# Tokens stationary in the last product, and one 512-column matmul over high and low operand in the front and the latents

## The chip, the cores and the metric

The kernel runs on one core of one Trainium2 chip. The time is device microseconds (us) of that core. The kernel before was run three times: 1950.55, 1955.09 and 1958.80 us, median 1955.09 us. The engines are named as in the profile: PE (TensorE matmuls), PEld (its weight loads), DVE (VectorE), ACT (ScalarE), POOL (GpSimd) and SP (the engine that issues most DMAs).

## The reference, cut to what matters

Two blocks follow one another on 256 tokens of width 2048, all in float32. The first normalises `x`, multiplies it by a wide input matrix, runs three mixers and an output product, and then attends to a memory of 256 rows. The second runs a pooling layer and a latent-attention layer on the tokens and on a context of 256 rows. What the change touches:

```
# front: memory's keys and values; the first columns of the mixers' input product
k, v = split(rms_norm(mem, mem_norm_g) @ wkv)
p = rms_norm(x, mix_norm_g) @ w_in
...
# every layer of the second block; the gate of the context is not used in the last layer
shift, scale, gate = split(silu(c) @ ada_w[i] + ada_b[i], 3)
c_q, c_kv, k_r, g = split(h @ mla_w_in)
o = attend(...)                                  # 16 heads of 128
y = (o * silu(g)) @ mla_w_out                    # 256 x 2048
x = x + gate * rms_norm_2(y, post_norm[i])       # the output, last layer
```

## The kernel before, in words

**Layout.** Activations lie transposed: a tile of `BIG` is 128 features by 256 tokens. A weight product reads its matrix in chunks of 512 rows by 512 columns (1 MB, two DMAs into `RAW`), and splits each chunk: ACT rounds it into `HI` (`act_high`, L306), DVE subtracts that from the raw values into `LO` (`dve_low`, L316), a half of 128x1024 elements at a time. The operand is split too, `x[:, 0, :]` the high part and `x[:, 1, :]` the low part, 256 tokens each (`XS`, `PS`). Each 128x128 block of weights gives three matmuls into one PSUM bank (`pe_block`, L489): high weights by high operand (L503), high weights by low operand (L504), low weights by high operand (L505). With one sequence (`seqs == 1`) each moves 256 columns, with two sequences (latent tokens and context) 512.

**Order.** Each engine has a queue of its own, written out by hand, and semaphores join them. `HI` and `LO` have two slots, so that the work on a chunk runs one to two chunks ahead of PE. PE signals `chunk_done` after each half of a chunk and `tile_done` after a finished output tile. A finished bank is evacuated: by ACT for the kinds `copy1`, `copy2`, `gain1` (`act_evac`), by DVE for `add1`, and by both for `gate1` (ACT writes a sigmoid of the bank, DVE multiplies it with the bank). A bank is used again only after that (`pe_bank`, L507).

**Beside it** the modulation vectors `silu(c) @ ada_w` and `silu(c_ctx) @ ada_w` are summed on DVE: 192 units of 512 KB, each with four operations of 128x512 (two k by two vectors, L427 and L431, `dve_unit`). After eight units PE adds the partitions up (`pe_ada`, L440, two matmuls with `PICK`). The last four slabs, units 160 to 191, are the gates of the last layer, and their units run in the attention stage.

**Stages the change touches.** *Front* (0 to 260 us): products `kv` (8 chunks), `win_a` (24), `win_b` (4, three tiles wide), all `copy1`; a barrier (`stage_end`) closes it. *Latents* (1338 to 1563 us): `cq` (4 chunks, `copy1`), `mg01` (8, `gate1`), `ckv`, `kr` (two sequences), `mg23` (8, `gate1`), then a barrier. *Pairs* (1563 to 1847 us): attention of two heads beside the products `uq` and `ukv` of the next two, nine rounds of some 32 us; in the ninth the first three chunks of the last product `mo` lie beside the attention. *mo* (1847 us to the end): the other 13 chunks, weights stationary, 256 tokens moving, result features by tokens. ACT takes each tile out twice (times the gate, L385, and squared, L388), DVE sums the squares (L2929), PE turns the input `x` (L2889, eight turns of four transposes) and the result (L2899, four calls of eight transposes) back to tokens by features and sums the squares over partitions (L2970), and DVE forms `x + y * rstd` in eight pieces (L2950), each sent out by SP.

## Time and profile before

| | us |
|---|---|
| median of three runs | 1955.09 |
| time of the profiled execution | 1950.72 |
| its span, first to last instruction | 1948.9 |
| PE busy | 1802.2 |
| DVE busy | 1416.7 |
| ACT busy | 817.5 |
| mean granted TensorE clock, share of full | 0.964 |

A row of a timeline gives start, duration, engine, line, operation, output and inputs, shapes and a count, and in brackets how long the engine had been idle and what released it. The ends of matmuls are modelled, so PE's pace is read from the starts of matmuls, not from their durations. The granted clock is a share of 2.4 GHz.

### The profile page before, as it was taken

The page shows a single profiled execution, that of the slowest core. Times are in us where ns is not written, and L with a number is a line of the kernel's source. Part 1 is how long each engine was busy: PE and PEld are TensorE (multiplying, and loading weights), DVE is VectorE, ACT ScalarE, POOL GpSimd, SP SyncE. Part 2 cuts the span into 40 slices and gives each one's busy share as a digit, 9 for nine tenths or more (in the row PEclk, how much of TensorE's full clock was granted, in tenths as well). Part 3 has the DMA queues.
Part 4 walks back from the last instruction along what each step waited for, and adds up shares of the span by engine and source line. Part 5 has one row for each costly group of instructions (what it writes and reads, how often), then busy time and mean ns, then how long its engine had stood idle before and what let it go on. Part 6 is the DMA issues. An engine that isn't in the chain of part 4 may idle for free.

```text
span 1948.9 us, 27051 instructions
## 1 busy us (share of the span) xinstructions
PE 1802.2 (92%) x10641; PEld 1547.9 (79%) x10641; DVE 1416.7 (73%) x2242; ACT 817.5 (42%) x1294; POOL 7.2 (0%) x18
## 2 busy tenths in 40 slices
PE   6999988997888888999999999997989999999897
PEld 6899988987777777877777777775978966667697
DVE  5788758778899677887688768777772677777443
ACT  6544365624435444233332223224453444444353
POOL 1000000000000000000000000000000000000000
PEclk9999999999899989999999999998999999999999
DMA  6577744535566344345455536553442453434243
GB/s 213 191 260 260 229 154 152 184 97 171 193 227 227 109 150 126 113 141 173 135 197 183 191 129 204 185 192 107 130 138 76 145 170 110 136 109 150 78 152 98
DMA packets 169000, 311.11 MB, mean 160 GB/s; under 512 B 14908, under 2 KB 23464, under 8 KB 168872
## 3 DMA queue, kind: packets, MB, share of 16 engines
q1 hardware_dynamic: 162176, 305.70, 48.0%
q10 hardware_dynamic: 6248, 3.62, 0.7%
q8 instruction: 84, 1.38, 0.3%
q14 instruction: 44, 0.36, 0.1%
q0 software_dynamic: 448, 0.06, 0.0%
HBM read 307.23 MB, written 2.10 MB: 159 GB/s over the span
## 4 chain that ended last, share of the span: by engine, by line
PE 52%; DVE 7%; ACT 3%; issue 1%; DMA 0%; DVEq 0%; ACTq 0%
PE bank L503 15%; PE bank L504 15%; PE bank L505 15%; DVE w_low L316 2%; PE bank L2627 2%; PE bank L2626 1%; DVE ada_acc L431 1%; PE bank L2646 1%; PE bank L449 1%; ACT w_high L306 1%; PE bank L2637 1%; DVE big L682 1%; DVE big L2470 0%; DVE big L2469 0%; DVE operand L677 0%
## 5 line engine op out<-in xcount | busy, mean ns | idle before, releaser
L503 PE MATMUL bank<-operand,w_high 128*128 128x256 f32 (+1 forms) x2704 | 872.4, 323 | 73.1 <-DVE w_low L316 43.5
L504 PE MATMUL bank<-operand,w_high 128*128 128x256 f32 (+1 forms) x2704 | 860.2, 318 | 0.0
L505 PE MATMUL bank<-operand,w_low 128*128 128x256 f32 (+1 forms) x2704 | 860.1, 318 | 0.0
L503 PEld LDWEIGHTS bank<-operand,w_high 128*128 128x128 f32 x2704 | 529.5, 196 | 130.7 <-DVE w_low L316 50.2
L316 DVE TENSOR_TENSOR w_low<-raw,w_high 128x1024 fp32r<-128x1024 f32 (+4 forms) x416 | 454.1, 1127 | 187.9 <-ACT w_high L306 186.4
L306 ACT ACTIVATE w_high<-raw 128x1024 fp32r<-128x1024 f32 (+4 forms) x416 | 394.5, 980 | 426.7 <-PE bank L505 216.7
L504 PEld LDWEIGHTS bank<-operand,w_high 128*128 128x128 f32 x2704 | 529.5, 196 | 30.2
L505 PEld LDWEIGHTS bank<-operand,w_low 128*128 128x128 f32 x2704 | 528.9, 196 | 30.5
L431 DVE SCALAR_TENSOR_TENSOR ada_acc<-ada_raw,silu_c,ada_acc 128x512 f32<-128x512 f32 x720 | 489.2, 745 | 7.0 <-DMA ada_raw<-in_ada_w 4.7
L503 PE MATMUL bank<-operand_small,w_high 128*128 128x512 f32 (+1 forms) x320 | 123.6, 386 | 5.4 <-DVE big L414 3.3
L504 PE MATMUL bank<-operand_small,w_high 128*128 128x512 f32 (+1 forms) x320 | 119.7, 374 | 0.0
L505 PE MATMUL bank<-operand_small,w_low 128*128 128x512 f32 (+1 forms) x320 | 119.3, 373 | 0.0
L503 PEld LDWEIGHTS bank<-operand_small,w_high 128*128 128x128 f32 x320 | 61.5, 192 | 24.5 <-DVE w_low L316 5.3
L505 PEld LDWEIGHTS bank<-operand_small,w_low 128*128 128x128 f32 x320 | 61.6, 192 | 10.9
L504 PEld LDWEIGHTS bank<-operand_small,w_high 128*128 128x128 f32 x320 | 61.7, 193 | 9.2
L2716 ACT ACTIVATE big<-bank,small 128x512 f32<-128x512 f32 x32 | 22.1, 690 | 107.2 <-DVE small L2783 107.2
L427 DVE TENSOR_SCALAR ada_acc<-ada_raw,silu_c 128x512 f32<-128x512 f32 x48 | 21.1, 482 | 61.1 <-PE bank L449 60.8
L351 ACT ACTIVATE big<-bank 128x256 f32<-128x256 f32 x87 | 33.0, 384 | 72.2 <-PE bank L505 71.3
L2782 DVE TENSOR_REDUCE small<-bank 128x1 f32<-128x512 f32 x32 | 22.1, 689 | 50.0 <-PE bank L2627 50.0
L361 ACT ACTIVATE big<-bank 128x512 f32<-128x512 f32 x53 | 31.4, 599 | 61.5 <-PE bank L505 61.3
L667 ACT ACTIVATE operand<-big,modulations 128x256 fp32r<-128x256 f32 x64 | 30.8, 505 | 42.0 <-DVE big L682 41.8
L449 PE MATMUL bank<-ada_acc,row_picker 128*48 128x512 f32 x80 | 41.5, 644 | 6.3 <-DVE ada_acc L431 6.3
(372 smaller groups left out, 1384.3 us busy)
## 6 DMA issues: line engine op xcount, KB each, us to landing
ada_raw<-in_ada_w SPq DMA_DIRECT2D x192, 512.0 KB, 4.0
raw<-in_w_in SPq DMA_DIRECT2D x96, 512.0 KB, 5.0
raw<-in_pool_w_in SPq DMA_DIRECT2D x64, 512.0 KB, 5.2
raw<-in_mla_w_in SPq DMA_DIRECT2D x48, 512.0 KB, 4.5
raw<-in_w_out SPq DMA_DIRECT2D x32, 512.0 KB, 5.7
raw<-in_pool_w_out SPq DMA_DIRECT2D x32, 512.0 KB, 5.9
raw<-in_mla_w_out SPq DMA_DIRECT2D x32, 512.0 KB, 4.2
raw<-in_xa_wkv SPq DMA_DIRECT2D x16, 512.0 KB, 4.7
```

What stands on the lines that cost most here:

```text
L306: ins = nc.scalar.activation(view(HI[:, slot, ks, :], False), view(RAW[:, slot, ks, :], True), ACT.Copy)
L316: ins = nc.vector.tensor_sub(view(LO[:, slot, ks, :], False), view(RAW[:, slot, ks, :], True), view(HI[:, slot, ks, :], False).bitcast(F32))
L351: nc.scalar.activation(dest_ap(p, i, n), PB[p.bank[i, n]][:, 0:T], ACT.Copy).then_inc(act_freed, 1)
L361: nc.scalar.activation(d, src, ACT.Copy).then_inc(act_freed, 1)
L431: ins = nc.vector.scalar_tensor_tensor(ACC[:, v], ARAW[:, us, k], SC[:, v, 2 * part + k:2 * part + k + 1], ACC[:, v], ALU.mult, ALU.add)
L449: ins = pe.matmul(PB[4][0:48, :], PICK[:, 47 - r:95 - r], ACC[:, v, :], start=b == 0 and v == 0, stop=b == 19 and v == 1, skip_group_check ...
L503: pe.matmul(out_, hi, x[:, 0, :], start=first, stop=False, skip_group_check=True)
L504: pe.matmul(out_, hi, x[:, 1, :], start=False, stop=False, skip_group_check=True)
L505: return pe.matmul(out_, lo, x[:, 0, :], start=False, stop=last, skip_group_check=True)
L667: nc.scalar.activation(n["dst"](k, 0), hf_tile(n, k), ACT.Identity, bias=n["shift"](k)).then_inc(xh_ready, 1)
L2627: la_pe.inc(pe.matmul(bank[:, :], BIG[r, q_of(a)[2], qt * P:(qt + 1) * P], KRT[r, :], start=False, stop=True), "s", a, u)
L2716: la_act.inc(s(PP[u % 2], PB[5 + u % 2][:, :], ACT.Exp, bias=m[:, 0:1], scale=mla_scale, accum_out=m[:, 1:2]), "e", a, u)
```

## The change

Four parts:

- **Wide matmul.** `kv`, `win_a`, `win_b`, `cq` (kind `sum1`) and `mg01`, `mg23` (kind `sumgate1`) send high and low operand through PE in one matmul of 512 columns. High sums lie in the left half of the bank, low sums in the right half, and DVE adds the halves with one `tensor_reduce` for each tile. ACT no longer evacuates these products. For the gates ACT writes the sigmoid of the summed tile into PSUM, and DVE multiplies.
- **Tokens stationary in `mo`.** 128x128 blocks of the operand are loaded as weights, and `HI` and `LO` move, 512 columns wide. The result is tokens by features, so it isn't turned. Its squares are summed along the row by ACT, DVE multiplies it by the gates in that layout. The last chunk is worked token half by token half.
- **Gates of the last layer as rows.** Only the vector of `c` is summed in units 160 to 191 (two operations instead of four). PE sums the partitions with a matmul by `ones`, which leaves the row in all 128 partitions (L452 of before). POOL fetches bias and gain rows, spread to 128 partitions, in eight DMAs of 256 KB, once `mg23` is done. DVE makes the gates in two operations of 128x512 for each slab.
- **Order.** In the front DVE's evacuations stand behind the `dve_low` of the next chunk; that of `win_b` stands behind the first `dve_low` of the next stage, and ACT's `act_high` for it no longer stands behind an evacuation. In the latents `cq` is evacuated by DVE behind the first `dve_low` of `mg01`.

```diff
-    kv = Product("kv", wkv, 4, 2, 4, 1, "copy1", half=1, dest=XAK, banks=5)
-    win_a = Product("win_a", w_in, 4, 6, 4, 1, "copy1", dest=LX)
-    win_b = Product("win_b", w_in, 4, 1, 3, 1, "copy1", dest=LX + 24, col0=6 * GW)
+    kv = Product("kv", wkv, 4, 2, 4, 1, "sum1", half=1, dest=XAK, banks=5)
+    win_a = Product("win_a", w_in, 4, 6, 4, 1, "sum1", dest=LX)
+    win_b = Product("win_b", w_in, 4, 1, 3, 1, "sum1", dest=LX + 24, col0=6 * GW)
...
-    mo = Product("mo", mw_out, 4, 4, 4, 1, "gain1", dest=32, banks=4)
+    mo = Product("mo", mw_out, 4, 4, 2, 1, "token", width=GW, banks=4)
...
         def dve_evac(dve, p, i, only=None):
+            if p.two_sums:
+                for n in range(p.tiles):
+                    wait_tile(dve, p, i, n)
+                    both = PB[p.bank[i, n]][:, :].rearrange("p (s t) -> p t s", s=2)
+                    nc.vector.tensor_reduce(dest_ap(p, i, n), both, AX.X, ALU.add).then_inc(
+                        dve_freed if p.kind == "sum1" else gate_summed, 1)
+                if p.kind == "sum1":
+                    return
...
-                elif p.kind == "gate1":
-                    wait_tile(act, p, i, n)
-                    nc.scalar.activation(dest_ap(p, i, n), PB[p.bank[i, n]][:, 0:T], ACT.Sigmoid).then_inc(gate_ready, 1)
+                elif p.kind == "sumgate1":
+                    act.wait_ge(gate_summed, p.sum0 + p.tiles * i + n + 1)
+                    nc.scalar.activation(PB[p.bank[i, n]][:, 0:T], dest_ap(p, i, n), ACT.Sigmoid).then_inc(gate_ready, 1)
...
+            sides = 2 if u < 160 else 1
             for k in range(2):
-                for v in range(2):
+                for v in range(sides):
...
+            if b >= 20:
+                ins = pe.matmul(PB[3][:, :], ones[:, :], ACC[:, 0, :], start=True, stop=True)
...
+        def pool_gate_rows(pool):
+
+            pool.wait_ge(chunk_done, 2 * (mg23.chunk0 + mg23.chunks * mg23.groups))
+            for q in range(4):
...
+                pool.dma_start(GATE_BIAS[q], halves(bias).to_broadcast([P, 2, T])).then_inc(gate_rows_in, 16)
+                pool.dma_start(GATE_GAIN[q], halves(gain).to_broadcast([P, 2, T])).then_inc(gate_rows_in, 16)
...
+            gate_dve.inc(nc.vector.tensor_tensor(GATE[q], halves(PB[3][:, :]), GATE_BIAS[q], ALU.add), "b", q)
+            gate_dve.inc(nc.vector.tensor_tensor(GATE[q], GATE[q], GATE_GAIN[q], ALU.mult), "g", q)
...
-            pe.matmul(out_, hi, x[:, 0, :], start=first, stop=False, skip_group_check=True)
-            pe.matmul(out_, hi, x[:, 1, :], start=False, stop=False, skip_group_check=True)
+            if p.two_sums:
+                pe.matmul(bank[:, :].rearrange("p (s t) -> p s t", s=2), hi, x, start=first, stop=False, skip_group_check=True)
+            else:
+                pe.matmul(out_, hi, x[:, 0, :], start=first, stop=False, skip_group_check=True)
+                pe.matmul(out_, hi, x[:, 1, :], start=False, stop=False, skip_group_check=True)
             return pe.matmul(out_, lo, x[:, 0, :], start=False, stop=last, skip_group_check=True)
...
             dve_low(dve, kv, 1, 0)
+            dve_evac(dve, kv, 0)
...
-            dve_product(dve, win_a)
-            dve_product(dve, win_b)
+            dve_product(dve, win_a, former=kv)
+            dve_product(dve, win_b, former=win_a)
             dve_low(dve, win_c, 0, 0)
+            dve_evac(dve, win_b, 0)
...
                     dve_low(dve, mg01, i, j)
+                    if i == 0 and j == 0:
+                        dve_evac(dve, cq, 0)
...
+        def pe_tokens(pe, i, j):
...
+                bank = PB[mo.bank[i, n]][:, :]
+                for k in (2 * h, 2 * h + 1):
+                    x = XS[:, KC * j + k, :, n * P:(n + 1) * P]
+                    pe.matmul(bank, x[:, 0, :], HI[:, slot, k, :], start=j == 0 and k == 0, stop=False, skip_group_check=True)
+                    pe.matmul(bank, x[:, 0, :], LO[:, slot, k, :], start=False, stop=False, skip_group_check=True)
+                    ins = pe.matmul(bank, x[:, 1, :], HI[:, slot, k, :], start=False, stop=j == 3 and k == 3,
+                                    skip_group_check=True)
...
+            for h in range(2):
+                act_squares(act, 3, h)
+                end_dve.wait(act, "s", h)
+                end_act.inc(s(RT[:, h:h + 1], RT[:, h:h + 1], ACT.Sqrt, bias=EPS, scale=1.0 / D), "r", h)
...
+                nc.vector.tensor_tensor(halves(YT[:, h, cols]), halves(PB[mo.bank[i, h]][:, :]), GATE[i], ALU.mult).then_inc(dve_freed, 1)
...
+            for h in range(2):
+                end_act.wait(dve, "q", 3, h)
+                end_dve.inc(v.tensor_reduce(RT[:, h:h + 1], SQS[:, h, :], AX.X, ALU.add), "s", h)
+                dve_by_gates(dve, 3, h)
+                end_act.wait(dve, "r", h)
+                end_dve.inc(v.reciprocal(RT[:, h:h + 1], RT[:, h:h + 1]), "r", h)
...
+                for i in range(4):
...
+                    v.scalar_tensor_tensor(XT[:, h, cols], YT[:, h, cols], RT[:, h:h + 1], XT[:, h, cols],
+                                           ALU.mult, ALU.add).then_inc(out_ready, 1)
```

## Rows read from the trace of the kernel before

**Rows 1.** The page's first part: busy time and instructions of each engine.

```profile
PE 1802.2 (92%) x10641; PEld 1547.9 (79%) x10641; DVE 1416.7 (73%) x2242; ACT 817.5 (42%) x1294; POOL 7.2 (0%) x18
```

**Rows 2.** Timeline of PE in `win_a`: first and last of 84 matmuls of 256 columns.

```profile
180.04 0.28 PE L503 MATMUL bank<-operand,w_high 128*128 128x256 f32 x1
...
190.00 0.28 PE L505 MATMUL bank<-operand,w_low 128*128 128x256 f32 x1
```

**Rows 3.** Timeline of PE in `ckv` and `kr`: first and last of 193 starts, 512 columns.

```profile
1458.15 0.39 PE L503 MATMUL bank<-operand,w_high 128*128 128x512 f32 x1
...
1501.67 0.39 PE L503 MATMUL bank<-operand,w_high 128*128 128x512 f32 x1
```

**Rows 4.** Windows in `mo`: length, busy time (count) by engine, then granted clock, DMA.

```profile
1847.00:1850.00 3.00, 3.00 (x14) 3.00 (x15) 2.21 (x2) 0.00 (x0) 0.00 (x0) 0.50 0.31 48
1856.00:1859.00 3.00, 2.56 (x14) 2.59 (x15) 0.00 (x0) 3.00 (x10) 0.00 (x0) 0.67 0.00 0
```

**Rows 5.** The page's groups of instructions: DVE's reduction of a whole bank.

```profile
L2782 DVE TENSOR_REDUCE small<-bank 128x1 f32<-128x512 f32 x32 | 22.1, 689 | 50.0 <-PE bank L2627 50.0
```

**Rows 6.** Timeline of DVE in `win_a`, from a new slab of the modulation sums.

```profile
168.25 0.88 DVE L427 TENSOR_SCALAR ada_acc<-ada_raw,silu_c 128x512 f32<-128x512 f32 x2 [5.30 <-PE bank L449]
...
172.64 2.73 DVE L431 SCALAR_TENSOR_TENSOR ada_acc<-ada_raw,silu_c,ada_acc 128x512 f32<-128x512 f32 x4
175.29 2.35 DVE L316 TENSOR_TENSOR w_low<-raw,w_high 128x1024 fp32r<-128x1024 f32 x2
...
177.56 2.73 DVE L431 SCALAR_TENSOR_TENSOR ada_acc<-ada_raw,silu_c,ada_acc 128x512 f32<-128x512 f32 x4
```

**Rows 7.** Timeline in `kv`: DVE's operand work, and the last chunk on PE.

```profile
66.07 1.23 DVE L879 TENSOR_TENSOR operand<-big,operand 128x1024 fp32r<-128x1024 f32 x1 [2.47 <-ACT operand L824]
...
86.61 0.58 PE L503 MATMUL bank<-operand,w_high 128*128 128x256 f32 x1 [3.22 <-DVE w_low L316]
```

**Rows 8.** Timeline at the barrier behind the front, DVE and PE.

```profile
258.15 2.36 DVE L316 TENSOR_TENSOR w_low<-raw,w_high 128x1024 fp32r<-128x1024 f32 x2 [8.10 <-ACT w_high L306]
...
260.66 0.55 PE L503 MATMUL bank<-operand,w_high 128*128 128x256 f32 x1 [3.91 <-DVEq L933]
```

**Rows 9.** Timeline of the latents, DVE, ACT and PE.

```profile
1386.66 1.23 DVE L2470 TENSOR_TENSOR big<-big 128x1024 f32<-128x1024 f32 x1
1391.39 2.36 DVE L316 TENSOR_TENSOR w_low<-raw,w_high 128x1024 fp32r<-128x1024 f32 x2 [3.51 <-ACT w_high L306]
...
1422.86 0.48 ACT L2430 ACTIVATE big<-bank,small 128x256 f32<-128x256 f32 x1 [3.79 <-PE bank L2530]
...
1450.29 0.50 PE L503 MATMUL bank<-operand,w_high 128*128 128x512 f32 x1 [3.44 <-DVE big L405]
...
1561.62 1.41 DVE L405 TENSOR_TENSOR big<-big,bank 128x256 f32<-128x256 f32 x4
```

**Rows 10.** The chain of work in a round of the pairs: start, us, what.

```profile
1610.49 0.66 PE bank L2637 x4
...
1614.78 1.85 PE bank L452 x4
```

**Rows 11.** Timeline of `mo` and the end, PE and DVE.

```profile
1846.91 0.55 PE L503 MATMUL bank<-operand,w_high 128*128 128x256 f32 x1 [2.24 <-ACT operand L2734]
...
1856.44 0.36 PE L503 MATMUL bank<-operand,w_high 128*128 128x256 f32 x1 [1.72 <-ACT big L388]
...
1869.95 0.60 PE L2889 MATMUL bank<-ident,big 128*128 128x128 f32 x4
1870.38 1.04 PE L2899 MATMUL bank<-ident,big 128*128 128x128 f32 x8
...
1937.30 1.06 PE L2899 MATMUL bank<-ident,big 128*128 128x128 f32 x8 [0.89 <-issue]
...
1943.57 1.40 DVE L2950 SCALAR_TENSOR_TENSOR big<-bank,small,big 128x512 f32<-128x512 f32 x2
```

**Rows 12.** The page's DMA issues: the eight output transfers, KB each, us to landing.

```profile
out<-big SPq DMA_DIRECT2D x8, 256.0 KB, 3.1
```

More of the change, by code:

```diff
@@ L73, in plan @@
                     continue
-                bank = n if p.banks == 4 else RINGS[p.banks][turn % len(RINGS[p.banks])]
+                bank = 2 * (i % 2) + n if p.kind == "token" else n if p.banks == 4 else RINGS[p.banks][turn % len(RINGS[p.banks])]
                 turn += 1
@@ L560, in pe_tile @@
                 ins.then_inc(tile_done, 1)
-        rs = gates = 0
+        rs = gates = sums_ = 0
         for p in products:
+            if p.kind == "sumgate1":
+                p.sum0 = sums_
+                sums_ += p.tiles * p.groups
             if p.kind == "gate2":
@@ L830, in act_front @@
             act_high(act, kv, 1, 0)
-            act_evac(act, kv, 0)
             high(0)
@@ L2417, in act_latents @@
                     act_high(act, mg01, i, j)
[L2418 to L2422 removed]
+                    if i == 1 and j == 0:
+                        act_evac(act, mg01, 0)
                     if i == 0:
@@ new lines, in build, with part @@
+        end_dve = steps("end_dve", [(x, h) for h in range(2) for x in ("s", "r")])
+        def pe_tokens(pe, i, j):
+            c = mo.chunk0 + 4 * i + j
+            slot, end = c % 2, (i, j) == (3, 3)
+            def part(h, n):
+                if j == 0 and h == 0:
+                    pe_bank(pe, mo, i, n)
+                    if (i, n) == (1, 1):
+                        gate_dve.wait(pe, "b", 3)
+                bank = PB[mo.bank[i, n]][:, :]
[5 more added lines that the diff above has]
+                                    skip_group_check=True)
+                return ins
+            if end:
+                for n in range(2):
+                    for h in range(2):
+                        pe.wait_ge(lo_ready, 2 * c + h + 1)
+                        ins = part(h, n)
+                    if n:
+                        ins.then_inc(chunk_done, 2)
+                    else:
+                        ins.then_inc(tile_done, 1)
+                return
+            for h in range(2):
+                pe.wait_ge(lo_ready, 2 * c + h + 1)
+                ins = part(h, 0)
+                if h == 1 and j == 3:
+                    ins.then_inc(tile_done, 1)
+                part(h, 1).then_inc(chunk_done, 1)
```

189 lines of the change are left out of this document (71 added, 118 removed).

## The prediction

> **What bounds it now.** I read the page first: PE is busy for 92% of the span, DVE for 73%, ACT for 42% [rows 1]. So PE's pace is the first term and DVE's queue the second. Then I listed PE's idle gaps over the timeline. In `win_a` and `win_b` (92 to 256 us) there is none that a transfer or DVE causes. In the latents the gaps end on DVE, and in the pairs they are under a microsecond. Last I read the starts of matmuls. At full clock 84 matmuls of 256 columns start within 190.00 - 180.04 us, 0.120 us apart [rows 2]. Matmuls of 512 columns start (1501.67 - 1458.15)/192 = 0.2267 us apart [rows 3]. Two of 256 take 0.240 us, one of 512 takes 0.2267 us: 0.0133 us are won for each pair made one. At half clock 14 matmuls of 256 columns fill 3.00 us, 0.214 us each [rows 4], which is 256 columns at 1.2 GHz, so there a pair made one should win nothing.
>
> The sum is made against the profiled execution's span, 1948.9 us. Its time was 1950.72 us, 4.4 us under the median of 1955.09 us; I apply the difference to the median.
>
> **Front, PE.** A chunk of four tiles and four k has 16 pairs: 48 x 0.120 = 5.76 us becomes 5.55 us. `win_a`, 24 chunks: -5.1 us. `win_b`, 4 chunks of 12 pairs: -0.6 us. This counts only if DVE keeps up. The page has one reduction of a whole bank, 0.69 us [rows 5]; the new one reads as many elements and writes 256 instead of one. Behind each other such operations start a little closer, so I take 0.66 us. DVE's work on a chunk of `win_a` is 177.56 - 172.64 = 4.92 us [rows 6]; with four reductions each fourth chunk it becomes 4.92 + 0.66 = 5.58 us, against PE's 5.55 us plus 1.85 us for `pe_ada` in each eighth chunk [rows 10], 5.78 us on the mean. That is a tie within 4%. But in every second group DVE already idles 5.3 us for the slab [rows 6], and it waits there for the tiles that it must reduce anyway. In the others the delay of some 3.6 us after a chunk's start falls by 0.6 us a chunk, and the low weights still come about 0.7 us before PE wants them. So PE stays the bound, and I take the full gain.
>
> **Front, `kv`.** Here DVE feeds PE: its `L879` idles 2.47 us for ACT, which had evacuated `kv` [rows 7]. Now DVE does it, four reductions paced by PE's tiles until about 65.3 us, and then the two normalisations that used to be done by 63.6 us. ACT gets earlier to its operand, but `L879` starts at about 67.7 instead of 66.07 us: 1.6 us, which reach the last chunk of `kv` (86.61 us, where PE waits 3.22 us for DVE [rows 7]). Less 0.2 us for that chunk: +1.4 us. The evacuation of the second group falls into idle time of DVE before 96 us.
>
> **Barrier.** ACT's rounding of the first chunk of `win_c` used to stand behind the evacuation of `win_b`, so DVE's low weights came at 258.15 us and PE restarted at 260.66 us, after 3.91 us of idle [rows 8]. Now rounding and subtraction are done while PE works; behind PE's last matmul stand only 0.3 us of signal and one reduction. The gap becomes about 1 us: -3.0 us. The bounds are 0 (if something else in the next stage was late) and -3.9.
>
> **Latents.** Here DVE and ACT pass work to and fro, and PE waits for them. (a) `cq`: DVE finished its update of the context at 1387.9 us and idled 3.51 us [rows 9]; the update, two operations of 1.23 us, was covered by that wait. Now the four reductions stand ahead of it, until 1389.2 us (the last tile comes at 1388.3, since PE gains 0.85 us in four chunks), so the update is uncovered: +2.5 us. (b) In `mg01`, second group, four reductions (2.6 us) stand ahead of the multiplications that free the banks; the square root that waited 3.79 us for PE [rows 9] comes later by these, less 0.3 us: +2.35 us. PE's gain in the eight chunks vanishes in its waits. (c) `ckv` waits 3.44 us for those banks [rows 9]. Four reductions more, but ACT's table load of 1.3 us, which the multiplications waited for, now runs beside them: +1.4 us. (d) `mg23`: -0.85 us on PE against +0.75 us for one reduction and multiplications that all come behind it: -0.1 us. (e) DVE's last work is the multiplications at 1561.62 us [rows 9], and everyone waits for it at the barrier; four reductions in front: +2.6 us. Together +8.75 us.
>
> **Pairs.** One matmul with `ones` instead of two: the four slabs take 1.85 us each on PE [rows 10], and now 0.93: -3.7 us. DVE's unit of 2.7 us becomes 1.35 us. It stood ahead of the reciprocal on which the transposes at 1610.49 us wait 0.18 us [rows 10], once in each of eight rounds: -1.4 us. The other 45 us that DVE saves lie beside PE and are worth nothing. The gates cost DVE 0.7 us more per slab, in an idle stretch of 2.8 us. At the start DVE waits for loads of units; shorter units free their buffers sooner: -0.5 us. The eight gate rows are 2 MB. A 256 KB transfer lands in 3.1 us [rows 12]; eight one after another would last 25 us. They are needed 50 us later, but share the engines with the unit loads. Those have 3 us of slack; I take 0 and keep +5 as the bound. The three chunks of `mo` beside the ninth round save 0.32 us each, half of it real: -0.5 us.
>
> **Last product.** Before, from 1846.91 to the end of PE's matmuls at 1937.30 - 0.89 = 1936.4 us: 89.5 us [rows 11]. After: a chunk is 24 x 0.2267 = 5.44 us instead of 5.76. The first one starts at half clock as before [rows 4], 7.0 us; 12 x 5.44 = 65.3; eight turns of `x` at 1870.38 - 1869.95 = 0.43 [rows 11], 3.4; two waits for ACT at these turns stay, 3.4. Sum 79.1: -10.4 us. Of these 4.2 are columns. The rest is the turns of `y`, the row turn, the 1.72 us wait for ACT's first evacuation at 1856.44 us, which waited for the gates, and the half clock after it (0.67 granted in that window [rows 4]).
>
> **Tail.** Before, from 1936.4 to 1948.9: 12.5 us. The last eight pieces end on DVE at 1943.57 + 1.40 us [rows 11], then the last transfer. After, the first token half is finished 2.7 us before PE ends, and its four pieces (0.66 us each) run until 2.3 us after; then come sum, gate product, reciprocal and four pieces, until 6.2 us after; and the last transfer as before (3.9 us): 10.1. -2.5 us.
>
> Sum: -5.7 + 1.4 - 3.0 + 8.75 - 3.7 - 1.4 - 0.5 - 0.5 - 10.4 - 2.5 = -17.6 us. Span 1931 us, profiled time 1933 us, median **1937 us**.
>
> **A rule beside the rows.** The Trainium skill (TensorE: Matmul & The Clock Gate, section Part 1: The HAM clock gate) gives bf16 matmuls at full clock N/2.4 GHz plus about 2.5 ns, and N/1.2 GHz exactly when cold. By it a pair made one would win 2.5 ns, not the 13.3 that [rows 2, 3] give, and the sum would come to about 1946 us, near the second rival below. The rows' excess is 0.120 - 0.1067 = 13.3 ns at 256 and 0.2267 - 0.2133 = 13.4 ns at 512 columns, a fixed cost in both, so the trace disagrees in size and agrees in form.
>
> **Rivals.**
> - *The reduction is dearer* (chance 0.09 between 0.85 and 1.1 us, 0.04 above). It reads two far halves of a bank for each result, which no row shows. At r us each, 24 reductions on the path (20 in the latents, 4 in `kv`) cost r - 0.66 more, and above 0.85 us DVE becomes the bound of `win_a`, 24 reductions more. At 1.23 us, what an operation on 1024 elements takes [rows 9], that is 24 x 0.57 + 24 x 0.38 = 22.8 us: 1960 us, slower. It decides from 1.12 us on; slower by 0.5% needs 1.33 us. Against it speaks that 512 elements of a bank were read in 0.69 us [rows 5].
> - *The pair made one wins nothing at full clock either* (0.06), as at half clock [rows 4]: if the fixed 13 ns goes with each run of 256 columns. Then `win_a` and `win_b` give back 5.7 us, the last product 4.7 and the latents 0.9: 1948 us. Against it speaks that 512 columns in one run show the 13 ns once [rows 3].
> - *Gate rows crowd out the loads at the start of the pairs* (0.08): +5 us, 1942 us.
> - *DVE in the latents costs double* because each uncovered reduction also shifts a table load or a bank (0.10): +8 us, 1945 us.
> - The forecast, -12 to -24 us: 0.63.
>
> **Numbers.** Half a per cent, 9.8 us, is about what a measurement can tell from no change. The limit of faster lies at 1945.3 us. Forecast, gate rows and half of the latents' rival lie below it, with some of the dearer reduction: faster 0.79. Same 0.16, slower 0.05. Range: the barrier's bound, -0.9 and +3.0; the start, +5; the tail and the waits in `mo`, 3 either way; the dearer reduction at 0.85 us, +4.6. Down to 1926 us and up to 1948 us.
>
> **What would show it.** PE starts 0.227 us apart in `win_a` with alternating single ones of 0.120; L316 of DVE still ahead of PE there; about 1 us of idle behind the front; in the latents the restart of the pairs 8 to 9 us later relative to their start; PE's chunks in `mo` 5.44 us apart and no wait of 1.7 us at its second chunk; the span ending 10 us after the last matmul. Wrong would make it a reduction above 0.85 us, PE waits on DVE in `win_a`, or a clock that falls to half where the gaps have moved.

## The result, and the profile after

The changed kernel takes **1939.19 us** (median of 7 runs, 1934.15 to 1942.83), the kernel before 1951.23 us in the same comparison (7 runs, 1947.02 to 1958.80): a ratio of 0.9932, 95% interval 0.9918 to 0.9946. It is faster, by 12.0 us or 0.7%. The forecast was 1937 us, but from a median of 1955.09 us that lay 3.9 us above the median of seven; that the two times are only 2 us apart is therefore partly luck. As a difference it promised 18 us, and 12.0 is the edge of its -12 to -24. The profiled spans are 1948.9 and 1935.7 us, so 13.2 us of the forecast's 17.6 are there. The single steps missed by more than their sum did.

The page of the changed kernel shows PE with fewer instructions, POOL's queue q0 with 2.15 MB (0.06 MB before), and the wide matmuls as a group of 880:

```profile
PE 1782.6 (92%) x9329; PEld 1474.0 (76%) x9329; DVE 1416.8 (73%) x2229; ACT 796.9 (41%) x1234; POOL 13.1 (1%) x26
q0 software_dynamic: 1088, 2.15, 0.4%
L520 PE MATMUL bank<-operand,w_high 128*128 128x512 f32 x880 | 320.4, 407 | 27.8 <-DVE w_low L321 16.9
```

L520 is the wide matmul, L524 the narrow one behind it. PE's share is the 92% of [rows 1], DVE's the 73%. Such shares can't say where 13 us went. For that I read landmarks on PE in both timelines: the start of the last chunk of `kv`, the restart behind the front's barrier, the first matmul with `ones` ahead of the latents, the restart of the pairs, the first chunk of `mo` that waits for its operand, and the end of `mo`'s matmuls (before, where the last transposes of the result follow, the 1936.4 us of the forecast). The last stage runs from there to the end of the span. Stage lengths between them, in us:

| kernel | to `kv`'s last chunk | to barrier | middle | latents | pairs | `mo` | tail |
|---|---|---|---|---|---|---|---|
| before | 86.6 | 174.05 | 1077.7 | 224.79 | 283.74 | 89.5 | 12.5 |
| after | 88.6 | 165.56 | 1075.5 | 234.10 | 282.56 | 81.1 | 8.2 |
| forecast of the difference | +1.4 | -8.7 | 0 | +8.75 | -6.1 | -10.4 | -2.5 |
| difference | +2.0 | -8.5 | -2.2 | +9.3 | -1.2 | -8.4 | -4.3 |

**Front.** The timeline of PE inside `win_a` (start, duration, line):

```profile
180.75 0.40 PE L520 MATMUL bank<-operand,w_high 128*128 128x512 f32 x1
180.99 0.28 PE L524 MATMUL bank<-operand,w_low 128*128 128x256 f32 x1
181.10 0.40 PE L520 MATMUL bank<-operand,w_high 128*128 128x512 f32 x1
...
182.16 0.40 PE L520 MATMUL bank<-operand,w_high 128*128 128x512 f32 x1
```

From 180.75 to 182.16 us are four wide and four narrow: 0.353 us for one of each, where [rows 2] and [rows 3] gave 0.2267 + 0.120 = 0.3467. PE never waits for DVE there; two slabs' matmuls, eight chunks apart, start as follows:

```profile
117.05 1.92 PE L456 MATMUL bank<-ada_acc,row_picker 128*48 128x512 f32 x4
...
211.58 1.92 PE L456 MATMUL bank<-ada_acc,row_picker 128*48 128x512 f32 x4
```

That is 94.53 us for 16 chunks, where the kernel before took 214.32 - 118.11 = 96.21. The gain is 1.68 us, for 256 pairs, 6.6 ns each and not 13.3. Over the 432 pairs of `win_a` and `win_b` that makes 2.9 us; the stage became 8.5 us shorter. The barrier has its 3.0 us, as forecast (the reductions on DVE, then PE's restart, against 3.91 us of idle in [rows 8]):

```profile
251.90 2.10 DVE L401 TENSOR_REDUCE big<-bank 128x256 f32<-128x512 f32 x3
254.15 0.36 PE L522 MATMUL bank<-operand,w_high 128*128 128x256 f32 x1 [0.88 <-DVEq L956]
```

What is left, some 2.6 us, is the clock. The windows from 80 to 100 us (length, busy times of PE, PEld, DVE, ACT and POOL, then the granted clock, DMA share, GB/s), first of before:

```profile
80.00:90.00 10.00, 6.78 (x45) 6.58 (x44) 8.17 (x8) 5.51 (x6) 0.00 (x0) 0.78 0.57 183
90.00:100.00 10.00, 10.00 (x76) 10.00 (x76) 6.06 (x8) 4.50 (x7) 0.00 (x0) 0.88 0.77 272
```

and of after:

```profile
80.00:90.00 10.00, 7.47 (x44) 6.31 (x43) 7.75 (x8) 5.91 (x6) 0.00 (x0) 1.00 0.53 164
90.00:100.00 10.00, 10.00 (x59) 8.69 (x58) 9.46 (x12) 3.19 (x3) 0.00 (x0) 1.00 0.82 275
```

The same stretch of work runs partly at the lower level before and wholly at the upper one after. The kernel with the old front (below) tells the two apart: it ran this stretch at 1.00 and took 171.5 us, 2.5 less than the kernel before. No step of the forecast said so.

**`kv`.** The reductions, DVE's step towards the operand, and PE's wait, which answer to [rows 7]:

```profile
63.02 2.77 DVE L401 TENSOR_REDUCE big<-bank 128x256 f32<-128x512 f32 x4 [1.09 <-PE bank L524]
...
68.06 1.23 DVE L900 TENSOR_TENSOR operand<-big,operand 128x1024 fp32r<-128x1024 f32 x1
...
88.59 0.50 PE L520 MATMUL bank<-operand,w_high 128*128 128x512 f32 x1 [2.53 <-DVE w_low L321]
```

The operand step came at 68.06 us, forecast 67.7, before 66.07. The last chunk is 2.0 us later, 0.6 of which the two profiles differ by already at 31 us, where PE turns the input.

**Latents.** Reductions of `cq`, the low weights that wait for ACT, then PE's waits at the bank of `mg01`, behind it, at `ckv`, at the end, to be read against [rows 9]:

```profile
1376.12 2.77 DVE L401 TENSOR_REDUCE big<-bank 128x256 f32<-128x512 f32 x4 [1.09 <-PE bank L524]
...
1383.57 2.36 DVE L321 TENSOR_TENSOR w_low<-raw,w_high 128x1024 fp32r<-128x1024 f32 x2 [2.29 <-ACT w_high L311]
...
1411.11 0.50 PE L520 MATMUL bank<-operand,w_high 128*128 128x512 f32 x1 [3.44 <-DVE big L409]
1426.81 0.50 PE L520 MATMUL bank<-operand,w_high 128*128 128x512 f32 x1 [2.39 <-DVE w_low L321]
1447.43 0.80 PE L522 MATMUL bank<-operand,w_high 128*128 128x512 f32 x1 [4.55 <-DVE big L409]
1559.83 2.48 DVE L401 TENSOR_REDUCE big<-bank 128x256 f32<-128x512 f32 x4
1563.78 0.55 PE L522 MATMUL bank<-operand,w_high 128*128 128x256 f32 x1 [4.25 <-DVEq L956]
```

A reduction takes 0.69 us. Four that wait for nothing take 2.48 us, (2.48 - 0.69)/3 = 0.60 us apart, where I had put 0.66. In `kv` and `cq` four take 2.77 us, since each waits for PE to finish its tile.

**Pairs.** Their start: POOL's first, fourth and last issue of a gate row, DVE's wait for a unit load, PE's wait for DVE:

```profile
1559.83 0.77 POOL L483 DMA_DIRECT2D scratch<-in_ada_b  x1 [1551.18 <-PE bank L524]
...
1566.95 0.72 POOL L484 DMA_DIRECT2D scratch<-in_post_norm  x1 [4.88 <-issue]
...
1577.73 0.72 POOL L484 DMA_DIRECT2D scratch<-in_post_norm  x1
1585.73 1.54 DVE L436 SCALAR_TENSOR_TENSOR ada_acc<-ada_raw,silu_c,ada_acc 128x512 f32<-128x512 f32 x2 [5.18 <-DMA ada_raw<-in_ada_w]
1588.64 1.15 PE L2649 MATMUL bank<-big 128*128 128x512 f32 x2 [2.89 <-DVE big L2631]
```

The kernel before reached its fourth pair of score matmuls (L2649; number 3 counted from nought, the third in the expectations) 40.84 us behind the barrier, the changed one 46.69: 5.85 us are lost in this stretch, and from there to `mo` 7.0 are won. The view of DMA issues from 1563 to 1590 us shows the loads (KB each, median us to landing), before:

```profile
ada_raw<-in_ada_w SPq DMA_DIRECT2D x4, 512.0 KB, 3.8
```

and after:

```profile
ada_raw<-in_ada_w SPq DMA_DIRECT2D x4, 512.0 KB, 7.8
scratch<-in_post_norm POOLq DMA_DIRECT2D x3, 256.0 KB, 6.6
```

**Last product and tail**, to be read against [rows 11]: the first chunk, two turns of `x`, one with a wait, DVE's last pieces.

```profile
1846.34 0.77 PE L2918 MATMUL bank<-w_high,operand 128*128 128x512 f32 x1 [2.24 <-ACT operand L2757]
...
1866.14 0.60 PE L2945 MATMUL bank<-ident,big 128*128 128x128 f32 x4
1872.07 0.60 PE L2945 MATMUL bank<-ident,big 128*128 128x128 f32 x4
1879.63 0.66 PE L2945 MATMUL bank<-ident,big 128*128 128x128 f32 x4 [1.47 <-ACT big L2965]
...
1930.19 2.74 DVE L2997 SCALAR_TENSOR_TENSOR big<-big,small 128x512 f32<-128x512 f32 x4
```

A chunk with its turn takes 5.93 us (forecast 5.87). The 1.72 us wait at the second chunk is gone. PE ends at 1927.47 us, DVE 5.5 us later, and the last transfer 2.8 us after that.

### The profile page after: what moved, and what is told of

Its sections match the earlier page's. It is cut to its first block, busy times and chain, and to the rows that moved or that the text cites. A ratio compares the mean times of both kernels' runs of the same rounds, so it can differ in the third digit from the quotient of the medians.

```text
span 1935.7 us, 24347 instructions
## 1 busy us (share of the span) xinstructions
PE 1782.6 (92%) x9329; PEld 1474.0 (76%) x9329; DVE 1416.8 (73%) x2229; ACT 796.9 (41%) x1234; POOL 13.1 (1%) x26
## 3 DMA queue, kind: packets, MB, share of 16 engines
q1 hardware_dynamic: 162176, 305.70, 48.5%
q0 software_dynamic: 1088, 2.15, 0.4%
## 4 chain that ended last, share of the span: by engine, by line
PE 54%; DVE 6%; ACT 2%; issue 1%; DMA 1%; DVEq 0%; ACTq 0%; SPq 0%
PE bank L524 14%; PE bank L522 13%; PE bank L523 13%; PE bank L520 2%; PE bank L2650 2%; DVE w_low L321 2%; PE bank L2918 2%; PE bank L2919 2%; PE bank L2920 2%; PE bank L2649 1%; PE bank L2669 1%; PE bank L456 1%; ACT w_high L311 1%; DMA ada_raw<-in_ada_w 1%; PE bank L2660 1%
## 5 line engine op out<-in xcount | busy, mean ns | idle before, releaser
L524 PE MATMUL bank<-operand,w_low 128*128 128x256 f32 (+1 forms) x2448 | 782.6, 320 | 0.0
L522 PE MATMUL bank<-operand,w_high 128*128 128x256 f32 (+1 forms) x1568 | 542.0, 346 | 51.2 <-DVE w_low L321 36.9
L523 PE MATMUL bank<-operand,w_high 128*128 128x256 f32 (+1 forms) x1568 | 532.6, 340 | 0.0
L524 PEld LDWEIGHTS bank<-operand,w_low 128*128 128x128 f32 x2448 | 474.5, 194 | 30.5
L436 DVE SCALAR_TENSOR_TENSOR ada_acc<-ada_raw,silu_c,ada_acc 128x512 f32<-128x512 f32 x660 | 452.1, 745 | 13.9 <-DMA ada_raw<-in_ada_w 10.4
L522 PEld LDWEIGHTS bank<-operand,w_high 128*128 128x128 f32 x1568 | 305.2, 195 | 100.7 <-DVE w_low L321 40.7
L520 PE MATMUL bank<-operand,w_high 128*128 128x512 f32 x880 | 320.4, 407 | 27.8 <-DVE w_low L321 16.9
L523 PEld LDWEIGHTS bank<-operand,w_high 128*128 128x128 f32 x1568 | 305.3, 195 | 30.8 <-issue 0.7
L520 PEld LDWEIGHTS bank<-operand,w_high 128*128 128x128 f32 x880 | 169.3, 192 | 74.4 <-DVE w_low L321 19.7
L524 PE MATMUL bank<-operand_small,w_low 128*128 128x512 f32 (+1 forms) x320 | 119.9, 375 | 0.0
L524 PEld LDWEIGHTS bank<-operand_small,w_low 128*128 128x128 f32 x320 | 62.0, 194 | 11.0
L2918 PE MATMUL bank<-w_high,operand 128*128 128x512 f32 x128 | 52.6, 411 | 2.4 <-ACT operand L2757 2.2
```

The source lines that it names most:

```text
L436: ins = nc.vector.scalar_tensor_tensor(ACC[:, v], ARAW[:, us, k], SC[:, v, 2 * part + k:2 * part + k + 1], ACC[:, v], ALU.mult, ALU.add)
L520: pe.matmul(bank[:, :].rearrange("p (s t) -> p s t", s=2), hi, x, start=first, stop=False, skip_group_check=True)
L522: pe.matmul(out_, hi, x[:, 0, :], start=first, stop=False, skip_group_check=True)
L523: pe.matmul(out_, hi, x[:, 1, :], start=False, stop=False, skip_group_check=True)
L524: return pe.matmul(out_, lo, x[:, 0, :], start=False, stop=last, skip_group_check=True)
L2918: pe.matmul(bank, x[:, 0, :], HI[:, slot, k, :], start=j == 0 and k == 0, stop=False, skip_group_check=True)
```

## The experiments

Twelve kernels ran, each an edit of the changed kernel. Each group of four was timed beside the kernel before on the same chip; its medians there were 1949.89, 1951.67 and 1951.08 us. Times are medians; stages are those of the table.

### Gate rows fetched early

```diff
-            pool.wait_ge(chunk_done, 2 * (mg23.chunk0 + mg23.chunks * mg23.groups))
+            pool.wait_ge(chunk_done, 2 * (kr.chunk0 + kr.chunks * kr.groups))
```

> The changed kernel, but POOL fetches the gate rows (eight DMAs of 256 KB) when the product kr is done, some 60 us earlier, beside mg23, which PE bounds. Theory: the rows crowd out a unit load at the start of the pairs (DVE idle 5.18 us for it at 1585.73 us, PE idle 2.89 us at 1588.64 us, then half clock). Then from the barrier to PE's third score matmul takes 46.7 us in the changed kernel and about 41 us here, and the whole becomes 5 to 6 us shorter (ratio to the kernel before about 0.990). Rival: the loads are late by themselves, since shorter units only ask for them sooner; then the wait stays and the time moves by less than 1 us. A second rival: the rows now delay the weights of mg23, and PE gets gaps there.

1932.24 us (1931.01 to 1934.48), ratio 0.9910 [0.9887, 0.9932], span 1930.9. The pairs fell from 282.56 to 275.72 us; the other stages moved by at most 1.6. The latents, where the rows now are, took 234.06 us and not 234.10, so the second rival is out. The waits that answer to the two above:

```profile
1585.30 1.54 DVE L436 SCALAR_TENSOR_TENSOR ada_acc<-ada_raw,silu_c,ada_acc 128x512 f32<-128x512 f32 x2 [2.84 <-DMA ada_raw<-in_ada_w]
...
1588.21 1.12 PE L2649 MATMUL bank<-big 128*128 128x512 f32 x2 [0.44 <-DVE big L2631]
```

PE's wait falls from 2.89 to 0.44 us, and the half clock behind it goes too. Windows of 3 us behind the wait, of after:

```profile
1588.60:1591.60 3.00, 2.96 (x4) 0.80 (x4) 0.00 (x0) 0.00 (x0) 0.00 (x0) 0.67 0.00 0
1591.60:1594.60 3.00, 3.00 (x14) 2.88 (x14) 2.63 (x4) 0.78 (x2) 0.00 (x0) 0.50 0.00 0
```

and of this version:

```profile
1588.20:1591.20 3.00, 2.99 (x11) 1.48 (x12) 0.69 (x1) 1.28 (x1) 0.00 (x0) 1.00 0.00 0
1591.20:1594.20 3.00, 3.00 (x13) 1.44 (x13) 2.91 (x5) 2.76 (x7) 0.00 (x0) 1.00 0.18 21
```

The fourth pair of score matmuls comes 41.18 us behind the barrier instead of 46.69. So the forecast's third rival was true: of the 5.85 us lost at the start 5.5 were the rows'. The Trainium skill (DMA: Bandwidth & Descriptors, section Queues, rings and completion order) says that each DMA engine takes turns between the queues that have work for it, packet by packet. The trace agrees in this: the unit load that SP issues 4.0 us behind the restart takes 9.2 us to land beside the gate rows and 6.6 us here. The medians of the four unit loads are 7.8 and 6.2 us; the rest of the way to the 3.8 us of before is not the rows' doing.

That one load separates all fourteen profiles, the median of four does not. POOL issues three rows, and the fourth only 0.39 us after the third has landed (in the changed kernel at 1566.56 and 1566.95 us). In seven profiles with late rows, the fourth to sixth row go out 3.0 to 5.1 us behind the restart, the load beside them takes 9.1 to 11.2 us, and the fourth pair of score matmuls comes after 44.2 to 47.4 us. In the other seven the load takes 6.2 to 6.6 us and the pair comes after 38.2 to 41.9.

### Latents without the reductions

In `cq`, `mg01` and `mg23` again two matmuls for the high weight, evacuated by ACT as before:

```diff
-    cq = Product("cq", mw_in, 4, 1, 4, 1, "sum1", dest=[32, 34, 36, 38], banks=6)
+    cq = Product("cq", mw_in, 4, 1, 4, 1, "copy1", dest=[32, 34, 36, 38], banks=6)
-    mg01 = Product("mg01", mw_in, 4, 2, 4, 1, "sumgate1", dest=GATES[0:8], col0=1088, banks=6)
+    mg01 = Product("mg01", mw_in, 4, 2, 4, 1, "gate1", dest=GATES[0:8], col0=1088, banks=6)
```

> The changed kernel, but cq, mg01 and mg23 as before: two matmuls of 256 columns for high and low operand, ACT evacuates. Theory: the wide matmul costs the latents time, because the reductions lie on DVE's path and PE waits there anyway; the stage took 224.8 us before and 234.1 us changed, and takes 225 us here; the whole is 9 us shorter than the changed kernel (ratio about 0.989). Rival: most of the 9 us comes from other parts (the clock, or where the stage happens to begin); then the stage takes 230 us or more. The three products' PE gain given up is 320 pairs of 13.3 ns, 4.3 us, if PE bounded them; if that counted, the gain would be about 5 us.

1921.27 us (1918.63 to 1924.51), ratio 0.9853 [0.9833, 0.9873]. The latents take 224.76 us, as before (224.79). PE's waits in them:

```profile
1411.18 0.39 PE L522 MATMUL bank<-operand,w_high 128*128 128x256 f32 x1 [1.04 <-DVE big L409]
1425.42 0.39 PE L522 MATMUL bank<-operand,w_high 128*128 128x256 f32 x1 [2.18 <-DVE w_low L321]
...
1444.95 0.50 PE L522 MATMUL bank<-operand,w_high 128*128 128x512 f32 x1 [3.44 <-DVE big L409]
```

The bank of `mg01` is waited for 1.04 instead of 3.44 us. The 9.3 us that the change lost here all come back. The pairs came out 5.7 us shorter too, though nothing in them was changed and the rows were still fetched late. POOL's fourth row, 6.4 us behind the restart and not 3.2:

```profile
1564.25 0.72 POOL L484 DMA_DIRECT2D scratch<-in_post_norm  x1 [7.59 <-issue]
```

Its third row had landed later, and the unit load issued 4.0 us behind the restart took only 6.3 us. This is read from the trace; no run moved those rows alone.

### Only cq without them

Gate rows early and only the `cq` line of the edit above.

> The kernel with early gate rows, and of the latents only cq back to four products of two matmuls, evacuated by ACT. The early-rows version took 234.06 us for the latents; with cq and both gate products as before it was 224.8. Theory, each product costs by itself what the prediction gave it: cq 2.5 us, so latents 231.6, span 1928.4 us. Rival, the waits in the two gate products take up what cq gives back: latents 234.0, span 1930.9. Other rival, the delay of cq is what makes the later waits: latents 228 or less.

1931.59 us (1928.58 to 1934.74), ratio 0.9903 [0.9888, 0.9918], span 1929.8. The latents took 233.36 us, so `cq` is worth 0.7 us and the gate products 8.6. None of the three expectations fits well; nearest is the one that `cq` gives nothing. The places where PE restarts, counted from the first matmul with `ones`, divide the rest:

| us from that matmul | after | only `cq` old | all old |
|---|---|---|---|
| bank of `mg01`'s second group free | 81.4 | 80.6 | 78.1 |
| low weights two chunks on | 97.1 | 96.3 | 92.4 |
| banks of `ckv` free | 117.8 | 116.9 | 111.9 |
| last wait in `mg23` | 209.6 | 208.8 | 202.6 |
| barrier | 234.1 | 233.4 | 224.8 |

Step by step the two gate products cost 2.4 + 1.5 + 1.1 + 1.2 + 2.4 = 8.6 us.

### Both together

> The changed kernel with the gate rows fetched early and with cq and both gate products in four tiles of two matmuls and no reduction, as before the change. The version without the reductions in the latents had a span of 1922.7 us, with a pairs stage of 276.84 us although its gate rows were still late; the version with early rows had 275.72 us. Theory, both gain from the same thing (the unit loads at the start of the pairs are not crowded, in the one because the rows are gone, in the other because they were issued 3 us earlier against the barrier): the gains don't add, the pairs take 275.5 to 276.8 us, the latents 224.8, span 1920.5 to 1922.7 us. Rival, the gains are separate and add: pairs 270 us, span 1916 us.

1919.62 us (1918.27 to 1923.77), ratio 0.9838 [0.9824, 0.9853], span 1922.0; pairs 275.95, latents 224.83. The gains don't add: beside the version without reductions, early rows are worth 0.9 us of pairs. The reason in the expectation does not hold: without the reductions POOL's first row went out 3.4 us ahead of the restart, in the changed kernel 4.0. What differed is when the fourth to sixth row meet the unit load, as above. With late rows the pairs took 281.3 to 282.6 us in six profiles, but 278.7 and 276.8 in two; with early rows and the shorter units 274.4 to 276.5 in all four.

### The front as before

`kv`, `win_a` and `win_b` with "copy1" again, evacuated by ACT.

> The changed kernel with kv, win_a and win_b as before the change (two matmuls of 256 columns for the high weight, evacuated by ACT); latents, pairs and last product stay changed. Theory, the front is worth what the landmarks of the two traces say: from the last chunk of kv to the barrier 174.0 us again instead of 165.6, and kv's last chunk 1.35 us earlier: +7.1 us, span 1942.8 us. If the 2.2 us that the middle of the program lost also came from the front's phases, +9.3 us, 1945.0. Rival, half of the 8.5 us is drift of the clock and not of the change: +3 us or less, 1939.

1946.27 us (1941.33 to 1948.04), ratio 0.9963 [0.9948, 0.9977], span 1946.3: 7.1 us slower than the changed kernel, 10.6 on the span. That the medians differ by just the expected 7.1 us confirms nothing, since the stages don't. From `kv` to the barrier it took 171.5 us and not the 174.0 expected, at a granted clock of 1.00 like the changed kernel: +6.0 us, of which 3.03 are at the barrier (start and wait as before):

```profile
257.58 0.36 PE L522 MATMUL bank<-operand,w_high 128*128 128x256 f32 x1 [3.91 <-DVEq L953]
```

and 2.9 are the columns. So of the stage's 8.5 us about 2.5 were clock, less than the half that the rival supposed. `kv`'s last chunk came 2.5 us earlier, at 86.06 us, 1.2 of which the profiles differ by already at 31 us. So the front makes 3.4 us of the span's 10.6. The rest arose where no code differs: 4.5 in the middle, 2.6 in the latents.

### The wide matmul split again in win_a

```diff
+            if p is win_a:
+                pe.matmul(bank[:, 0:T], hi, x[:, 0, :], start=first, stop=False, skip_group_check=True)
+                pe.matmul(bank[:, T:2 * T], hi, x[:, 1, :], start=False, stop=False, skip_group_check=True)
```

> The changed kernel, but in win_a the wide matmul is made as two of 256 columns into the two halves of the bank; the reduction on DVE stays. It isolates what one matmul for two wins. Theory: 384 pairs at 13.3 ns, win_a takes 5.1 us longer, the whole as well (ratio about 0.996). Rival: a pair made one wins 2.5 ns, or the front's gain came from the order of the evacuations; then less than 1.5 us. A second rival: DVE and PE are so nearly tied in win_a that a slower PE costs less than 5.1 us because waits vanish; then 2 to 4 us.

1940.95 us (1936.76 to 1944.48), ratio 0.9952 [0.9933, 0.9970]. The slab's matmuls start 48.1 us apart, as in the kernel before, against 47.26:

```profile
117.54 1.92 PE L456 MATMUL bank<-ada_acc,row_picker 128*48 128x512 f32 x4
165.66 1.92 PE L456 MATMUL bank<-ada_acc,row_picker 128*48 128x512 f32 x4
```

All of `win_a`'s 2.5 us come back, and only those: from `kv` to the barrier 168.1 us instead of 165.6. That is half of the expected 5.1. It is not the second rival either, since no wait of PE in `win_a` was there to vanish: the gain of a pair is 6.6 ns.

### Where the other half of the pair's gain is

Two changes of the matmuls in `win_a`, each with one time.

```diff
-                    for k in (2 * h, 2 * h + 1):
-                        ins = pe_block(pe, p, i, j, n, k)
+                        for part in range(2):
+                            for k in (2 * h, 2 * h + 1):
+                                ins = pe_block(pe, p, i, j, n, k, part)
```

> Only the order of matmuls in win_a is changed: for each tile and pair of k first the two wide ones, then the two narrow ones, instead of wide and narrow in turn. In the changed kernel one wide and one narrow start within 0.3533 us, where the rows of before gave 0.2267 + 0.120 = 0.3467. If the missing 6.7 ns go with each turn from one width to the other, half as many turns halve them: a tile's four then take 0.700 us instead of 0.7067, and eight chunks with their slab 46.8 us instead of 47.26. If they go with the wide matmul itself, whose moving operand and bank are two runs of 256 columns each, nothing moves: 0.7067 us and 47.26 us.

```profile
117.32 1.92 PE L456 MATMUL bank<-ada_acc,row_picker 128*48 128x512 f32 x4
...
210.63 1.92 PE L456 MATMUL bank<-ada_acc,row_picker 128*48 128x512 f32 x4
```

46.65 us for eight chunks: 0.61 less than in turn, and more than the half of 0.85 that was expected. The one time was 1933.00 us, span 1931.2, of which some 4 us are a shorter pairs stage.

```diff
+            if p is win_a:
+                pe.matmul(bank[:, :], hi, XS[:, kk % 8, 0, :], start=first, stop=False, skip_group_check=True)
```

> In win_a the wide matmul reads 512 neighbouring columns of the high operand (of a fixed set of tiles) instead of 256 of the high and 256 of the low one, 512 elements apart; so this product's values are not the reference's, all else runs as before. If the two runs cost the 6.7 ns, wide and narrow now start within 0.3467 us and eight chunks with their slab take 46.4 us instead of 47.26. If the turn from wide to narrow costs them, 0.3533 and 47.26 stay.

This kernel leaves the low operand out of the wide matmul. Eight chunks took 47.26 us, and a pair 0.353: the two runs of 256 columns cost nothing. One time, 1936.35 us, span 1934.6.

### Groups of eight, and the best of all

> The version with early gate rows and the latents as before the change (span 1922.0 us), and now in win_a all eight wide matmuls of a half chunk first, then its eight narrow ones (4 turns of width a chunk instead of 32), in kv and win_b wide and narrow grouped in twos. In the version that halved the turns eight chunks with their slab took 46.66 instead of 47.26 us. Theory, the turn is what costs: about 1.05 us for eight chunks, slab distance 46.2 us, with kv and win_b 3.3 us in all, span 1918.7 us. Rival, the four tiles now end within a microsecond of each other, DVE reduces later, and the barrier or kv gives it back: the span stays at 1921 to 1923 though the slab distance falls.

1919.90 us (1915.05 to 1921.20), ratio 0.9838 [0.9825, 0.9852], span 1918.4. Eight wide and eight narrow start within 2.79 us (0.349 a pair):

```profile
180.71 1.11 PE L527 MATMUL bank<-operand,w_low 128*128 128x256 f32 x8
181.66 2.00 PE L521 MATMUL bank<-operand,w_high 128*128 128x512 f32 x8
183.50 0.76 PE L527 MATMUL bank<-operand,w_low 128*128 128x256 f32 x5
```

but the slab's distance was 47.06 us, not 46.2: sixteen groups of 2.79 us and the slab's 1.92 make 46.6, and where the other half microsecond goes is open. The time equals that of the version before it. I take this as no gain.

### The reduction made twice

Each reduction of `win_a` is carried out a second time into the same tile.

```diff
+                    if p is win_a:
+                        nc.vector.tensor_reduce(dest_ap(p, i, n), both, AX.X, ALU.add).then_inc(reduced_once, 1)
+                        dve.wait_ge(reduced_once, p.tiles * i + n + 1)
                     nc.vector.tensor_reduce(dest_ap(p, i, n), both, AX.X, ALU.add).then_inc(
```

> The changed kernel, but each of the 24 reductions of win_a is done twice, about 1.3 us a tile instead of 0.6. It tests the break-even that I put at 0.85 us a tile. By that account win_a is bound by DVE: 24 times (1.3 - 0.85) = 11 us longer, PE shows waits for the low weights in each group. Rival: the waits for the slab in every second group absorb it, and only the other three transitions show; then 0 to 3 us longer.

1944.46 us (1938.39 to 1948.49), ratio 0.9970 [0.9956, 0.9984]. Two waits for DVE appear in `win_a`, the first of them followed by matmuls at the lower clock:

```profile
151.35 0.80 PE L524 MATMUL bank<-operand,w_high 128*128 128x512 f32 x1 [2.02 <-DVE w_low L322]
...
201.58 0.50 PE L524 MATMUL bank<-operand,w_high 128*128 128x512 f32 x1 [1.49 <-DVE w_low L322]
```

The stage takes 171.6 us against 165.6 and 167.0 in two profiles with single reductions: 4.7 to 6.1 us, between the two expectations (11, and 0 to 3). A tile now takes DVE 1.33 us instead of 0.60, 24 x 0.73 = 17.5 us more work. So at such a price DVE makes PE wait, as the forecast's first rival says, but only twice and not in each group; DVE's slack ahead of PE in `win_a` swallowed the other 12 us.

### Both vectors in the last units

```diff
-            sides = 2 if u < 160 else 1
+            sides = 2
```

> The kernel with early gate rows, and in the last 32 units DVE again multiplies both silu vectors, 2.74 us a unit instead of 1.54; the matmul with ones stays one. The early-rows version took 275.72 us for the pairs and 62.34 us for two of its rounds, the kernel before 64.36; the single matmul with ones explains 0.93 of these 2.02. Theory, the other 1.09 us are the shorter units, which stand on DVE ahead of steps that PE waits for: two rounds 63.4 us, pairs 280.1, span 1935.3. The prediction's own term for it is smaller, 0.18 us a round: pairs 277.1, span 1932.3. Rival, what DVE saves lies beside PE and is worth nothing: 275.7, span 1930.9.

1941.66 us (1932.21 to 1943.84), ratio 0.9944 [0.9925, 0.9962]. Two rounds take 63.16 us instead of 62.34, the pairs 279.36 instead of 275.72: the shorter units are worth 3.6 us there, near the 4.4 of the theory and not the 1.4 of the forecast (1.9 with its 0.5 for the start). The span is 10.5 us longer than with early rows alone; the other 7 lie in the middle (+4.1) and the latents (+2.6), whose code is the same.

### Reductions ahead of the low weights at the barrier

```diff
-            dve_low(dve, win_c, 0, 0)
             dve_evac(dve, win_b, 0)
+            dve_low(dve, win_c, 0, 0)
```

> The changed kernel, with DVE's reductions of win_b put ahead of the low weights of win_c's first chunk instead of behind them. Theory, what shortened the barrier from 3.91 to 0.88 us is that no rounding and no subtraction is left behind PE's last matmul; now half a chunk of subtraction, two operations of some 0.49 us, stands there again: the gap becomes 1.9 us, +1.0 us on the span. If all four operations of the chunk count, 2.9 us. Rival, the gap is short because ACT no longer evacuates anything, and DVE's order is worth nothing: 0.9 us.

1940.24 us (1937.52 to 1941.39), ratio 0.9945 [0.9934, 0.9957]. The restart:

```profile
259.42 0.36 PE L522 MATMUL bank<-operand,w_high 128*128 128x256 f32 x1 [3.15 <-DVEq L956]
```

The wait is 3.15 instead of 0.88 us, +2.27. I had expected 1.9 or 2.9 us of wait. The barrier waits until DVE has emptied its queue, so both halves of the chunk stand in it, 2.36 us by [rows 8]. So 2.3 of the 3.0 us rest on DVE's order. The other 0.8, from 3.15 to 3.91, go with ACT, which evacuates nothing here; no run tested that by itself.

## Why the prediction was right, and where not

In the order of its sum:

- **Front, PE: -5.7, measured -2.9.** The step that failed is "0.0133 us are won for each pair made one": 13.3 ns were 6.6. The rows of before showed each width by itself; nothing showed them in turn. In `kv` and `cq` a wide and a narrow do start within 0.347 us, in `win_a` and `win_b` within 0.353. Fewer turns win part of it back, one run of columns doesn't. Since the same turns cost nothing in `cq`, the turn alone is not the cause, and what is stays open. That split matmuls give the 2.5 us back is shown. The rule of the Trainium skill (TensorE: Matmul & The Clock Gate, section Part 1: The HAM clock gate), a fixed 2.5 ns a bf16 matmul, would as an estimate have given 1.1 us for the 432 pairs; the measured 2.9 lies between that and the 5.7 from the rows.
- **PE stays the bound of `win_a`: right.** No wait for DVE appeared, and one did when the reductions were doubled.
- **`kv`: +1.4, measured +1.35** without what the two profiles already differed by at its start.
- **Barrier: -3.0, measured -3.03**, all of it shown by the old front and 2.3 of it by the turned order.
- **Latents: +8.75, measured +9.3, but put together wrongly.** `cq` was forecast at 2.5 and cost 0.7: PE reached `cq`'s last tile 48.5 us into the stage against 50.2 in the version with `cq` old, with a clock that had come back sooner (0.71 against 0.50 in the first 6 us). I take it that this ate most of DVE's delay; no run shows it. The gate products were forecast at 6.25 and cost 8.6: the bank (2.4 against 2.35), `ckv` (1.1 against 1.4) and the end (2.4 against 2.6) were sized well. What I left out are the low weights behind the same four reductions in `mg01`, 1.5 us, and 1.2 us in `mg23`, where I had -0.1.
- **Pairs, start: -0.5 with the gate rows at 0; measured +5.85.** This is the step that failed most: "Those have 3 us of slack; I take 0 and keep +5 as the bound". The slack was not there: beside the fourth to sixth row a unit load took 9.2 us instead of 6.6, DVE waited 5.18 us for a later one, PE 2.89 us for DVE, and then PE ran at half clock, which the forecast had named as a sign of being wrong. Shown by fetching the rows early: -5.5 us in this stretch, -6.8 in the stage.
- **Pairs, rest: -5.6, measured -7.0.** The step that was sized wrong is the shorter units, put at 1.4 and worth 3.6 by the experiment; not only the 0.18 us wait before the transposes ends on DVE. The matmul with `ones` (3.7) had no run of its own; with both vectors but this one matmul two rounds took 63.16 us against 64.36 before, 1.2 us less where 0.93 were forecast.
- **Last product: -10.4, measured -8.4.** The first chunk ran at half clock for longer, 8.42 us where I took 7.0. In each of the eight chunks with a turn the first half's matmuls start some 0.232 us apart instead of 0.2267, together 0.5 us. The waits at turns were 2 x 1.47. About 0.5 us I can't place.
- **Tail: -2.5, measured -4.3.** DVE was done 5.5 us behind PE (forecast 6.2), and the last transfer took 2.8 us (forecast 3.9, as before).
- **Not in the sum: 4.8 us**, 2.6 in the front, which the granted clock and the old front show, and 2.2 in the middle, whose cause is open. The mean clock there rose from 0.961 to 0.967, but the version with early rows had 0.962 and the shortest middle of all. These 4.8 us are luck, and they covered most of what the gate rows cost.

So the total came within 5 us by errors of both signs, which is luck in part; the barrier, `kv`, the latents' total and PE as the bound of `win_a` were not. Of the four rivals one was true (gate rows), one was half true (the pair's gain); the dearer reduction and the latents at double cost were not.

## What to carry to other kernels

A trace that shows two shapes each by itself does not price their alternation: bound it. Transfers that are needed only much later still have to be placed; where a stage's start depends on loads that arrive only just in time, issue them in a stage with slack on DMA. And a fusion that saves PE 7 ns a pair but puts 0.6 us of reduction on the engine that PE waits for pays in a stage that PE bounds and costs in one that it doesn't: reverting it only in the latents, with the rows early, gives 1919.6 us, 19.6 us under the changed kernel. The two stages account for 15.9 of them in the profiles (9.3 in the latents, 6.6 in the pairs).

## What the runs showed of the hardware

- A wide and a narrow matmul in turn start within 0.353 us in `win_a`, 0.347 in `cq`, at the same granted clock of 1.00.
- A reduction over two far halves of a bank, 128x256 from 128x512, takes 0.69 us, as long as the one over neighbouring elements in [rows 5], and 0.60 us from start to start where nothing is waited for.
- POOL issued the eight 256 KB rows by threes: the fourth 0.39 us after the third had landed, the seventh 0.35 us after the sixth, in all thirteen profiles with rows.
- The middle, where no version changes an instruction, took 1074.8 to 1080.0 us in fourteen profiles, and the latents of equal code 234.1 or 236.7: between profiles of equal code some of the stretches at half clock come and go. From `kv` to the barrier, equal code took 165.6 us at a mean clock of 1.00 and 167.0 at 0.99. A difference of 3 us between two single spans of this kernel says nothing by itself; the stage that was edited has to show it.
